# Scores behind the transposes: the order of two matmul groups in the attention loops of a fused two-block kernel

## The reference

```python
s = jnp.einsum('bqhgd,bkhd->bhgqk', qi, k, preferred_element_type=F32) * scale
p = jax.nn.softmax(s, -1).astype(v.dtype)
return jnp.einsum('bhgqk,bkhd->bqhgd', p, v)
```

## Time and profile before

| | us |
|---|---|
| median of 3 runs | 2589.86 |
| lowest and highest | 2588.22, 2589.97 |
| the profiled execution's time | 2589.86 |
| its span in the profile | 2588.1 |
| TensorE busy | 2212.1 (85%) |
| VectorE busy | 1360.2 (53%) |
| ScalarE busy | 906.5 (35%) |
| GpSimd busy | 504.7 (20%) |

### The profile page before, as it was taken

How to read it: one execution, slowest core, us unless ns; L and a number is a source line. 1 busy time by engine, 2 the same in 40 slices (tenths; PEclk the granted TensorE clock), 3 DMA queues, 4 the chain that set the end, 5 groups by cost and what they waited for, 6 DMA issues and landing times.

```text
span 2588.1 us, 33786 instructions
## 1 busy us (share of the span) xinstructions
PE 2212.1 (85%) x13593; PEld 1669.5 (65%) x13593; DVE 1360.2 (53%) x2527; ACT 906.5 (35%) x1779; POOL 504.7 (20%) x457
## 2 busy tenths in 40 slices
PE   6979788869899776489898988779999987977998
PEld 5757566558466565389753444558888855546998
DVE  4548677563446999155443356453333333455554
ACT  3234454551212432154222244232222222344443
POOL 0047878420057950000000011000000000000000
PEclk8989899889899988599898988889999998998999
DMA  8254454643444329975541211332323332315553
GB/s 281 72 176 132 133 149 121 214 132 99 134 107 107 86 67 180 248 205 166 177 124 57 91 57 50 114 100 96 98 88 90 106 109 76 104 49 163 186 164 106
DMA packets 423666, 324.38 MB, mean 125 GB/s; under 512 B 65086, under 2 KB 411470, under 8 KB 422358
## 3 DMA queue, kind: packets, MB, share of 16 engines
q1 hardware_dynamic: 386452, 295.70, 39.2%
q10 hardware_dynamic: 34242, 16.92, 2.3%
q0 software_dynamic: 2816, 9.60, 1.1%
HBM read 292.42 MB, written 29.75 MB: 124 GB/s over the span
## 4 chain that ended last, share of the span: by engine, by line
PE 61%; DVE 13%; POOL 9%; ACT 6%; DMA 5%; issue 4%; SPq 1%; ACTq 1%; DVEq 0%; POOLq 0%
PE ps L119 59%; POOL A L88 8%; ACT A L115 3%; DVE A L88 2%; DMA wbuf<-ctab 2%; DVE R L88 2%; PE ps L122 2%; DVE A L102 2%; DVE A L92 1%; DVE A L105 1%; SPq L125 1%; DVE A L93 1%; DMA wbuf<-in_ada_w 1%; POOL A L125 1%; DVE A L96 1%
## 5 line engine op out<-in xcount | busy, mean ns | idle before, releaser
L119 PE MATMUL ps<-R,R 128*128 128x256 f32 (+1 forms) x3968 | 845.2, 335 | 35.3 <-ACT R L115 25.1
L119 PEld LDWEIGHTS ps<-R,R 128*128 128x128 f32 x3968 | 631.5, 193 | 109.6 <-ACT R L115 30.3
L119 PE MATMUL ps<-HR,R 128*128 128x512 f32 (+1 forms) x1984 | 555.3, 364 | 35.6 <-DVE R L88 24.8
L88 DVE TENSOR_TENSOR R<-wbuf,R 128x1024 fp32r<-128x1024 f32 (+2 forms) x304 | 332.2, 1101 | 376.3 <-ACT R L115 376.1
L115 ACT ACTIVATE A<-ps 128x512 f32<-128x512 f32 (+4 forms) x400 | 210.4, 556 | 613.4 <-PE ps L119 410.1
L119 PEld LDWEIGHTS ps<-HR,R 128*128 128x128 f32 x1984 | 357.1, 193 | 94.4 <-issue 28.6
L88 POOL TENSOR_TENSOR A<-A 128x512 f32<-128x512 f32 (+3 forms) x258 | 294.6, 1156 | 527.0 <-DVE A L96 267.0
L88 DVE TENSOR_TENSOR A<-A 128x128 f32<-128x128 f32 (+4 forms) x796 | 359.6, 482 | 62.8 <-ACT A L115 25.9
L115 ACT ACTIVATE R<-wbuf 128x1024 fp32r<-128x1024 f32 (+2 forms) x304 | 270.0, 894 | 291.1 <-PE ps L119 264.0
L119 PE MATMUL ps<-H,wbuf 128*128 128x512 f32 (+2 forms) x928 | 342.0, 527 | 13.8 <-DVE H L93 13.8
L119 PE MATMUL ps<-A 128*128 128x64 f32 (+10 forms) x1736 | 285.2, 364 | 34.6 <-DMA wbuf<-ctab 9.4
(11 more groups left out here) (102 smaller groups left out, 1624.5 us busy)
## 6 DMA issues: line engine op xcount, KB each, us to landing
wbuf<-in_w_ada SPq DMA_DIRECT2D x48, 1024.0 KB, 5.2
wbuf<-in_ada_w SPq DMA_DIRECT2D x24, 1024.0 KB, 9.7
wbuf<-in_w_out SPq DMA_DIRECT2D x24, 1024.0 KB, 5.6
wbuf<-in_w_ffn_gate SPq DMA_DIRECT2D x22, 1024.0 KB, 5.3
wbuf<-in_w_ffn_up SPq DMA_DIRECT2D x22, 1024.0 KB, 5.7
wbuf<-in_w_ffn_down SPq DMA_DIRECT2D x32, 704.0 KB, 4.7
wbuf<-in_attn_w_in SPq DMA_DIRECT2D x20, 1024.0 KB, 6.8
ctab<-A ACTq DMA_DIRECT2D x64, 256.0 KB, 2.8
```

Source lines behind the costliest of these rows:

```text
L88: return self.op(lambda e: e.tensor_tensor(out, a, b, op))
L119: return self.op(lambda e: e.matmul(out, lhsT, rhs, start=start, stop=stop, skip_group_check=True))
```

## The change

In the TensorE streams of both attention classes the two blocks of a step change places: the transposes of item i-2 come first, with the wait for their normalization, and the scores of item i after them. Both blocks are word for word as before; the other engines' streams are unchanged. The banks are now taken in the new order.

```diff
             def pe(self, pe):
                 N, nm = len(self.items), self.name
                 for i in self.steps:
-                    if i < N:
-                        it, key = self.items[i], (nm, i)
-                        p = PS.take(pe, (nm, "s", i), (dve_step, (nm, "m", i)) if it.mask is not None else (act_exp, key))
-                        for s, k in it.ready:
-                            pe.wait_ge(s, k)
-                        pe.mm(p[:, 0:it.n], it.q, it.k, True, True).then_inc(mm_done, (nm, "s", i))
                     if 2 <= i < N + 2:
                         it, key = self.items[i - 2], (nm, i - 2)
                         p = PS.take(pe, (nm, "t", i - 2), (act_evac, (nm, "t", i - 2)))
...
                         x.then_inc(tr_done, key)
+                    if i < N:
+                        it, key = self.items[i], (nm, i)
+                        p = PS.take(pe, (nm, "s", i), (dve_step, (nm, "m", i)) if it.mask is not None else (act_exp, key))
+                        for s, k in it.ready:
+                            pe.wait_ge(s, k)
+                        pe.mm(p[:, 0:it.n], it.q, it.k, True, True).then_inc(mm_done, (nm, "s", i))
                     yield
```

More of the change, by code:

```diff
@@ L2373, in pe @@
                 for i in self.steps:
+                    if 2 <= i < NI + 2:
+                        hp, qt, n = items[i - 2]
+                        key = (N, "at", i - 2)
+                        for hh in range(2):
+                            if hh == 0 or n == 512:
+                                p = PS.take(pe, (N, "t", i - 2, hh), (act_evac, (N, "t", i - 2)))
+                            at = 256 if hh and n == 256 else 0
+                            pe.wait_ge(dve_norm, key)
+                            for j in range(n // 128):
+                                x = pe.tr(p[:, at + j * 128:at + j * 128 + 128], PB[key][hh][:, j * 128:j * 128 + 128], ident)
+                        x.then_inc(tr_done, key)
                     if i < NI:
@@ L2385, in pe @@
                         x.then_inc(mm_done, (N, "s", i))
[L2386 to L2396, removed]
                     yield
```

## The result

The changed kernel took 2616.5 us (median of 4 runs, 2610.8 to 2618.6) against 2589.0 (4 runs, 2587.6 to 2590.0): a ratio of 1.0103, 95% interval 1.0085 to 1.0121. It is slower by 27.5 us, where the forecast said 12 on its base of 2589.86 and its range ended 23 above it.

The account below looks back on a forecast made before the run. The prediction took most of the program to run at the pace of TensorE's matmuls, busy 2212.1 of 2588.1 us. Its terms 8 + 4 - 2 + 2 = +12 on 2589.86 gave 2602 us, range 2588 to 2613.

Parts of the forecast that it names:

- Group 3, +8: First attention's last group: new order closes a loop of one item a turn instead of two; +8 us, bounds 4 and 11.
- the waits that were to show it: Group 3: VectorE's mask and maximum would wait for TensorE at nearly every item, 0.6 to 1.1 us each.
- Walking through it item by item with that filler between s(i) and t(i-1), and the lower clock up to 518: Group 3: reckoned VectorE's starts with ada-panel filler; item 15 at 561.0 against 553.13, so +7.9 us.
- The clock falls: Rival, chance 0.07: more idle in group 3 holds TensorE at 1.2 GHz; 8 us more, half on the path, 2606 us.
- 3 x 13.0 + 10.3 = 49.3: Group 3: sum of the loop's step prices from item 1 to item 15, 49.3 us against 45.2 before.
- 4 (the bare loop): Group 3: lower bound of the loss, 4 us, from the loop alone.
- Groups 0 to 2, +4: First attention's earlier groups: scores now follow TensorE's waits for the normalization; +4 us, bounds 0 and 10.
- Pair attention of layer 0, -2: Layer 0's pair attention: transposes run under waits for scarce PSUM banks; -2 us, bounds -5 and +2.
- +0.9 for two maxima: Layer 0's pair attention: two maxima on the chain start 0.45 us later, adding 0.9 us.
- Pair attention of layer 1, +2: Layer 1's pair attention: s(2) behind the waiting t(0) delays a maximum and exp(2); +2 us, bounds -1 and +4.
- Every wait counts: Rival, chance 0.08: all 12 waits and 9 late scores of groups 0 to 2 are paid; +20 us, 2610.
- Faster: Rival, chance 0.10: transposes slide under bank waits in layer 0's pair attention, -5 us, 2585 us.

Follow-up runs that it names:

- the first kernel with unread work: New order in group 3 alone, plus score products nobody reads in two of three steps, against the kernel before: ratio 1.0037.
- the second: The whole change plus the same score products nobody reads in group 3, against the kernel before: 2605.9 us, ratio 1.0066.
- the order alone: New order in group 3 without the unread score products, eight profiles: 55.0 to 60.8 us from item 1 to item 15, mean 59.2.
- the whole change in the third set: The whole change run once more against the kernel before, in a later set of runs on one chip: 2614.3 us, ratio 1.0099.
- group 3 alone in the fourth set: New order only in group 3 of the first attention, rerun in the last set against the kernel before: ratio 1.0061, median +18.8 us.

## Why the prediction was wrong in size

**Group 3, +8.** The mechanism was right: the waits that were to show it stand at every item of the profile after, though longer than the 0.6 to 1.1 us foretold (1.0 to 3.9). The step that failed is "Walking through it item by item with that filler between s(i) and t(i-1), and the lower clock up to 518". Its starts of items 1, 4, 8, 12 and 15 are 13.0, 17.2, 13.3 and 9.6 us apart, 53.1 in all. The profile after has 13.2, 18.0, 16.7 and 12.7; the first kernel with unread work has 12.1, 17.6, 14.1 and 10.0, 53.8 in all, the second 51.7 in all; the order alone took 59.2 on average. So the walk is right for a loop with the clock mostly up, and short from item 8 on: the lower clock doesn't end at 518. It comes back all through the group, because the loop itself leaves TensorE idle for 0.5 to 2.8 us at eleven of fourteen turns. Filling this idle time brought the clock from 0.73 to 0.84 up to about 0.9, and 6.5 us back (59.2 to 52.7, means of eight profiles and of two). That was the mechanism of the rival *The clock falls*, whose half on the path was 4 us; it got 0.07 as if it excluded the forecast, and it came on top of it. The other end of the difference was mis-sized too: the 45.2 us of the profile before are 41.2 in the five others, where TensorE came to its full clock earlier (0.57 from 505 to 522 in the profile before; 0.70 to 0.85 in the five). Against 41.2 the loop costs 11.5 us and the clock 6.5, together 18, for which the forecast had 8.

One sum beside the walk is wrong in itself: 3 x 13.0 + 10.3 = 49.3 counts fifteen turns, and from item 1 to item 15 there are fourteen, 3 x 13.0 + 2.8 + 3.8 = 45.6. So "4 (the bare loop)" should have been 0.4, and the other 7.5 us of the walk are filler and lower clock.

**Groups 0 to 2, +4.** Alone they gave 1.0005, with the pair attentions +4.1 us. The profiles say more when the time is taken from VectorE's first maximum of the attention (it stands at 171.29, so that the attention begins well ahead of the 240 given above) to item 1 of group 3. Before, then after:

```profile
171.29 0.42 DVE L105 TENSOR_REDUCE A<-ps 128x1 f32<-128x256 f32 x1 [1.80 <-PE ps L119]
```

```profile
170.17 0.42 DVE L105 TENSOR_REDUCE A<-ps 128x1 f32<-128x256 f32 x1 [0.39 <-PE ps L119]
```

Nine profiles with the new order in these groups take 334.1 to 343.4 us, mean 340.2; nine with the old order of matmuls there take 333.0 to 340.5, mean 337.4. That is about +3, near the forecast, with a spread as large as the effect.

**Pair attention of layer 0, -2.** The move is as described: in the changed kernel t(3) comes first and s(5) behind it has no wait, against 1.34 us, but the second wait of the earlier trace rows is as long as before:

```profile
1508.99 1.06 PE L122 MATMUL ps<-C,A 128*128 128x128 f32 x8 [0.95 <-ACT A L115]
1509.99 0.70 PE L119 MATMUL ps<-A 64*128 64x256 f32 x4
...
1541.51 1.97 PE L122 MATMUL ps<-C,A 128*128 128x128 f32 x8 [5.03 <-DVE A L88]
```

Measured from the first maximum (1473.58 before, 1487.68 after) to the first product's halves behind the layer's attention (1642.41, 1655.45), the profile after has -1.1 us; but the whole change in the third set has +1.8 (1489.66, 1660.33), and so have the pair attentions alone and three more kernels; of seven profiles with the new order there two have -1.1. The -1.1 holds a gain by the clock (0.88 in its 1544:1574, against 0.83 in the kernel before's 1530:1560 and 0.81 in the third set's 1548:1578). So the term is nearer +2 than -2. VectorE's starts show where it went: at 1501.97 of the kernel before all seven have gained the 1.1 us foretold as 1.5, and by 1531.64 all seven have lost 2.3 to 2.5, where the forecast had gains and +0.9 for two maxima; only behind that do the two part from the five, by 3 us up to 1553.03. Which wait makes the 2.4 wasn't followed up.

**Pair attention of layer 1, +2.** The late maximum is there as foretold: t(0) at 2253.39, the maximum of item 2 at 2255.59, 2.20 us behind it instead of 0.65, so 1.55 later (forecast 1.5).

```profile
2253.39 1.09 PE L122 MATMUL ps<-C,A 128*128 128x128 f32 x8 [1.57 <-DVE A L92]
...
2255.59 1.29 DVE L105 TENSOR_REDUCE A<-ps 128x1 f32<-128x512 f32 x2 [1.47 <-PE ps L119]
```

It didn't cost what the forecast took from it. Over the layer (2083.82 to 2329.17 on VectorE before) there are +0.3 us in the profile after and +3.5 in that of the third set, but both hold 2.9 us lost ahead of the attention, in unchanged code (last section). From 2192.61, behind that loss, all seven profiles are 2.1 us faster by 2269.15, the late maximum made up for and more; up to 2329.17 two have -2.6, four +0.5 to +0.6 and one -0.1. What parts -2.6 from +0.5 is again the clock. One stretch of about the same work: kernel before, changed kernel, changed kernel in the third set:

```profile
2260.00:2290.00 30.00, 26.27 (x176) 14.44 (x174) 17.41 (x41) 11.93 (x33) 1.76 (x4) 0.82 0.11 36
```

```profile
2277.00:2307.00 30.00, 22.89 (x176) 12.75 (x176) 20.08 (x49) 14.25 (x39) 2.13 (x5) 0.94 0.11 36
```

```profile
2284.00:2314.00 30.00, 23.81 (x152) 12.99 (x150) 17.89 (x43) 12.32 (x35) 1.79 (x4) 0.83 0.11 36
```

At 0.94 the same kernel does 176 matmuls in 30 us, at 0.83 152. Both layers together, with the 2.9 us, are -0.8 to +5.4 in the seven profiles, mean +3.3, forecast 0; the runs of them alone, 0.9999, can't tell these apart.

**The sum.** About +3, +15.5 to +18, and -1 to +5 are 18 to 26 us; three sets gave +15.8, +21.9 and +19.2 (group 3 alone +11.2 and +18.8). The 27.5 of the result stay above it: the profile there holds 13.1, and its four other runs, without a profile, 8 to 16 us more than that. Where these lie was not recorded. Nor do the terms add up to the 13.1 of the profile after: VectorE is 17.9 us late at 562 of the kernel before and 14.1 at the first pair attention, because from 851.00 to 1303.81, in the S5 layer, where no instruction changed, this execution was 3.9 us faster. In the other profiles the same stretch lies between 9.2 us faster and 4.2 slower than in the profile before, whatever the order. Other runs show only that single executions of one kernel differ by as much: group 3 alone took 2594.9 to 2616.2 us in the fourth set.

Of the other rivals, *Every wait counts* gave a time near the later sets but for a wrong reason, since groups 0 to 2 gave 3 and not 10, and *Faster* had its -5 in the place where two of seven profiles have -1.1 and five a loss.

## What to carry over

Where two engines hand an item back and forth, count how many items one turn of the loop spans before moving an instruction behind a wait; going from two items to one cost 0.8 us an item here (11.5 in 14), and one item more of distance gained 3.4 us of group 3 in the one profile of it, on the old order. Then price the idle time that the loop leaves: TensorE's lower clock in it cost more than half of what the loop did (6.5 us to 11.5), so the rival on the clock should be added to the sum rather than set beside it. And look at more than one profile for the base of a sum: the group that mattered here took 45.2 us in the one shown and 41.2 in five others.

## What the hardware showed

The granted clock can fall or hold after the same idle time. In the kernel before and in the changed kernel, at the same place, where no instruction differs, TensorE does two matmuls, idles 2.06 us (2.05) and does the next two; before, then after:

```profile
2125.28 1.10 PE L119 MATMUL ps<-A,C 128*128 128x512 f32 x2 [0.98 <-ACT A L115]
2128.43 1.10 PE L119 MATMUL ps<-A,C 128*128 128x512 f32 x2 [2.06 <-ACT A L115]
```

```profile
2139.21 1.10 PE L119 MATMUL ps<-A,C 128*128 128x512 f32 x2 [0.97 <-ACT A L115]
2142.36 2.05 PE L119 MATMUL ps<-A,C 128*128 128x512 f32 x2 [2.05 <-ACT A L115]
```

The second pair takes 1.10 us in the one and 2.05 in the other: it ran at 2.4 and at 1.2 GHz, behind the same instructions and the same pause. From there to the end of the 64 matmuls that follow, this cost 2.9 us (2143.18 and 2160.03 against the 13.93 by which the pairs were apart). The Trainium skill (TensorE: Matmul & The Clock Gate, A second HAM failure mode: psum-queue depth-cycling) has brief idling make the clock swing; the trace agrees that it swings, and adds that the same pause doesn't always do it. Nor does it fall evenly on the kernels: six of the seven profiles with the new order in the pair attentions lose 2.9 us by 2192.61 and the seventh 1.7, while of the eleven with the old order there only one loses (2.8, group 3 alone in the fourth set). Whether the new order in layer 0 brings this about wasn't tested.

In the profile of group 3 alone in the fourth set, the pair attention of layer 1, in its old order, was at 0.75:

```profile
2277.00:2308.00 31.00, 27.59 (x174) 15.44 (x172) 18.79 (x45) 12.17 (x34) 1.89 (x4) 0.75 0.11 35
```

From 2125.28 of the kernel before to its end, that execution lost some 12 us without a changed instruction. So a change of 0.2% in this kernel can't be read from one profile's total, and a term of the sum is best checked by the time between two instructions around it, in several.
